# First output projection: four pairs of modulation weights loaded first, the embeddings in other memory, and eight gate products moved under layer A's output tiles

## What is computed

```
y = concat([y_h, y_f])                        # 1024 + 1024 wide
h = x + y @ w_out                             # the first output projection
h = h + sigmoid(h @ w_ple_gate) * (p @ w_ple) # p: embeddings, 256 wide
h = rmsnorm(h, final_norm_w)
for layer i in (A, B):
    shift, scale, gate = split(silu(c) @ w_ada[i] + b_ada[i])          # for the tokens
    shift_c, scale_c, gate_c = split(silu(c_ctx) @ w_ada[i] + b_ada[i])# for the context
    u = h * (1 + scale) + shift
    h = layer_norm(ALPHA * h + gate * mixer_i(u), ...)
```

## Time and profile before

| | us |
|---|---|
| median of 3 runs | 3524.75 |
| lowest, highest | 3517.57, 3527.97 |
| the profiled execution's own time | 3509.49 |
| its span | 3507.7 |
| TensorE busy | 3189.2 (91%) |
| VectorE busy | 2024.5 (58%) |
| first output projection, first group of tiles | 1320.7 to 1410.4 |
| second group | 1425.1 to 1515.6 |
| embeddings' product | 1546.0 to 1569.8 |
| gate product starts | 1571.25 |

### The profile page before, as it was taken

One profiled execution on the slowest core, in us unless ns is written; L12 is line 12 of the kernel. 1 busy time (PEld: TensorE's weight loads), 2 busy tenths in 40 slices (PEclk: granted clock), 3 DMA queues, 4 the chain that ended last, 5 costly groups with the idle time before them and its releaser, 6 DMA issues.

```text
span 3507.7 us, 49113 instructions
## 1 busy us (share of the span) xinstructions
PE 3189.2 (91%) x18168; PEld 2659.5 (76%) x18168; DVE 2024.5 (58%) x3865; ACT 1288.3 (37%) x2277; POOL 877.3 (25%) x324
## 2 busy tenths in 40 slices
PE   7999999899999989869799989999779999999986
PEld 6878888777777768657588878887657777777765
DVE  4766657555566555965655545544455555555543
ACT  3433343344444440022344434430134444554402
POOL 2554444422222223334110010003111111111120
PEclk8999999999999999989899999999689999999996
DMA  2111111111111136541200010042021111110321
GB/s 98 52 39 45 36 39 41 65 44 65 49 54 49 55 144 252 191 142 44 97 34 28 28 40 28 28 167 91 12 77 47 41 47 47 41 35 31 119 96 60
DMA packets 64695, 236.95 MB, mean 68 GB/s; under 512 B 7024, under 2 KB 10096, under 8 KB 63488
## 3 DMA queue, kind: packets, MB, share of 16 engines
q1 hardware_dynamic: 31680, 115.91, 9.2%
q10 hardware_dynamic: 32832, 118.58, 9.1%
HBM read 184.06 MB, written 50.40 MB: 67 GB/s over the span
## 4 chain that ended last, share of the span: by engine, by line
PE 66%; DVE 16%; issue 5%; DVEq 5%; ACT 4%; DMA 2%; ACTq 1%; POOLq 1%; POOL 0%; SPq 0%
PE ps L1124 20%; PE ps L165 19%; PE ps L1189 4%; PE ps L1155 4%; PE ps L1171 4%; PE ps L727 3%; PE ps L120 3%; DVE x_in L1647 2%; PE ps L704 2%; DVEq L526 2%; PE ps L361 1%; DVE fox_l L1276 1%; PE ps L688 1%; DVE ctx_in L1647 1%; DVE h_sb L1647 1%
## 5 line engine op out<-in xcount | busy, mean ns | idle before, releaser
L186 POOL TENSOR_TENSOR w_hi<-raw,small 128x1024 fp32r<-128x1024 f32 x160 | 453.9, 2837 | 2528.8 <-PE ps L165 1335.5
L188 POOL TENSOR_TENSOR w_lo<-raw,w_hi 128x1024 fp32r<-128x1024 f32 x160 | 423.7, 2648 | 22.8
L1124 PE MATMUL ps<-nb_u_hi,w_hi 128*128 128x512 f32 (+1 forms) x640 | 252.0, 394 | 21.6 <-DVE nb_q_lo L2185 12.1
L1124 PE MATMUL ps<-nb_u_hi,w_lo 128*128 128x512 f32 (+1 forms) x640 | 248.2, 388 | 0.0
L1124 PE MATMUL ps<-nb_u_lo,w_hi 128*128 128x512 f32 (+1 forms) x640 | 247.2, 386 | 0.0
L1287 DVE TENSOR_TENSOR nb_pt_lo<-ps,nb_pt_hi 128x512 fp32r<-128x512 f32 x208 | 143.8, 691 | 143.0 <-ACT nb_pt_hi L1214 142.7
L165 PE MATMUL ps<-u_hi,w_hi 128*128 128x512 f32 x528 | 213.3, 404 | 7.8 <-DVE u_lo L245 7.8
L1124 PE MATMUL ps<-u_hi,w_hi 128*128 128x512 f32 x512 | 209.7, 410 | 4.5 <-POOL w_lo L188 4.5
L1124 PE MATMUL ps<-u_hi,w_lo 128*128 128x512 f32 x512 | 210.1, 410 | 0.0
L165 PE MATMUL ps<-u_hi,w_lo 128*128 128x512 f32 x528 | 210.0, 398 | 0.0
L1124 PE MATMUL ps<-u_lo,w_hi 128*128 128x512 f32 x512 | 208.9, 408 | 0.0
(11 more groups left out here) (348 smaller groups left out, 8121.5 us busy)
## 6 DMA issues: line engine op xcount, KB each, us to landing
raw<-in_w_stream SPq DMA_DIRECT2D x160, 512.0 KB, 3.2
h_sb<-in_w_ada ACTq DMA_DIRECT2D x12, 1024.0 KB, 4.8
ctx_in<-in_w_ada ACTq DMA_DIRECT2D x12, 1024.0 KB, 4.8
nf_b<-nf_rows ACTq DMA_DIRECT2D x16, 512.0 KB, 4.4
nb_bias<-in_rel_bias ACTq DMA_DIRECT2D x16, 448.0 KB, 3.6
y_parts<-wa_y_hi ACTq DMA_DIRECT2D x8, 640.0 KB, 3.0
y_parts<-wa_y_lo ACTq DMA_DIRECT2D x8, 640.0 KB, 4.1
la_out_yh<-y_parts SPq DMA_DIRECT2D x8, 640.0 KB, 10.0
```

The source lines that it names most:

```text
L186: pool.tensor_tensor(w_hi[:, s, :], raw[:, s, :], zero, ALU.add)
L188: pool.tensor_tensor(w_lo[:, s, :], raw[:, s, :], w_hi[:, s, :].bitcast(F32), ALU.subtract).then_inc(w_ready, 1)
L1124: mm = pe.matmul(ps[:, b:b + ch["n"]], w(slot, k), u[:, k, ch["c0"]:ch["c0"] + ch["n"]], start=k == 0 and p == 0, stop=k == KT - 1 and p == 2)
```

## The change

- The weights' pairs in the first projection are 20 instead of 24 (units 0 to 39). Pairs 0 to 3 are loaded at once into four slots, all in `h_sb`, pairs 4 to 15 into `h_sb[4:6]` and `h_sb[6:8]`, and pairs 16 to 19 into memory of `y_hi0`/`y_lo0` (a new view `rows4`), which ScalarE's queue may fill when the second group's HGRN tiles are done (`U_OUT + 12`). `cond` moves to the context's memory.
- For pairs 0 to 15 only the reductions for i = 0 are preceded by a drain. Pairs 16 to 19 keep both.
- `OUT1_ORDER`: additions 0 to 3 after 9, 10, 11 and 12 pairs, additions 4 to 7 after 16, 17, 18 and 19. `p_lo` is made before addition 6.
- `p` is loaded behind pair 15 into `r_hi[6:8]`'s memory. `p_hi` is `r_lo[4:6]` and `p_lo` is `r_lo[6:8]`, so VectorE's `r_lo[4]` to `r_lo[7]` wait for the embeddings' product (before: two of them).
- Units 40 to 47 (layer B's gates, i = 0) become eight reductions in `Layer.dve` of layer A, two each ahead of tiles 2, 3, 5 and 6. ScalarE's queue loads silu's input (0.5 MB) and two blocks of 2 MB for them, into memory that was a gap.

```diff
-        cond = h_sb[:, 4:6, :]
-        ada_pairs = [h_sb[:, 6:8, :], p_in.rearrange("p (u n) -> p u n", u=2)]
-        PAIRS_ADA = ADA_UNITS // 2
+        cond = ctx_in[:].rearrange("p k t -> p (k t)").rearrange("p (i n) -> p i n", i=2)
+        PAIRS_ADA = 20
         OUT1_ORDER = [("pair", p) for p in range(PAIRS_ADA)]
-        for k, pairs_before in enumerate((9, 10, 12, 13)):
-            OUT1_ORDER.insert(pairs_before + k, ("add", k))
-        OUT1_ORDER += [("add", k) for k in range(4, KT)]
+        for p, k in ((19, 7), (18, 6), (17, 5), (16, 4), (12, 3), (11, 2), (10, 1), (9, 0)):
+            OUT1_ORDER.insert(p, ("add", k))
+        OUT1_ORDER.insert(OUT1_ORDER.index(("add", 6)), ("low", 0))
...
+        p_raw = rows4[:, KT - 2:KT, :]
+        p_hi = r_lo[:, KT - 4:KT - 2, :]
+        p_lo = r_lo[:, KT - 2:, :]
+        def ada_pair(p):
+            if p >= 16:
+                return rows4[:, KT + 2 * (p % 2):KT + 2 * (p % 2) + 2, :]
+            first = (4, 6, 0, 2)[p] if p < 4 else (4, 6)[p % 2]
+            return h_sb[:, first:first + 2, :]
...
-            load_pair(0)
-            load_pair(1)
+            for p in range(4):
+                load_pair(p)
...
+                if what == "pair":
+                    nxt = {0: 4, 1: 5, 2: None, 3: None}.get(n, n + 2)
+                    if nxt and nxt < PAIRS_ADA:
+                        act.wait_ge(ada_done, n + 1)
+                        load_pair(nxt)
+                    if n == 15:
+                        act.dma_start(p_raw, a["p_t"]).then_inc(p_loaded, 16)
+                elif what == "add":
+                    if n + 1 < KT:
+                        act.wait_ge(o_added, n + 1)
+                        load_x(n + 1)
+                    if n == 4:
+                        act.wait_ge(p_loaded, 16)
+                        nc.scalar.copy(p_hi, p_raw).then_inc(p_hi_set, 1)
...
-                        for i, out in outs if 2 * n + j < ADA_UNITS - KT else outs[:1]:
-                            dve.drain()
+                        for i, out in ((0, x_in[:, 1, :]), (1, w if n < 16 else x_in[:, 1, :])):
+                            if i == 0 or n >= 16:
+                                dve.drain()
...
-                if k == KT - 2:
+                if k == KT - 4:
                     dve.wait_ge(w_used, U_PLE + 2)
...
+                residual(0)
+                if self.l == 0:
+                    act.dma_start(self.cond[:], a["cond"][0:1, :].broadcast_to([P, D])).then_inc(cond_loaded, 16)
+                    next_ada(0)
+                    act.wait_ge(cond_loaded, 48)
+                    nc.scalar.activation(self.cond[:], self.cond[:], ACT.Silu).then_inc(cond_set, 1)
+                residual(1)
+                if self.l == 0:
+                    next_ada(1)
...
+                    for j in range(2):
+                        w = self.ada_w[:, 2 * (step % 2) + j, :]
+                        dve.drain()
+                        ins = dve.tensor_tensor_reduce(self.ada_x[:], w, self.cond[:], 1.0, small[:, 0:1], ALU.mult,
+                                                       ALU.add, ada[:, 40 + 2 * step + j, 0:1])
...
+                    if l == 0 and k in (2, 3, 5, 6):
+                        dot_gates((2, 3, 5, 6).index(k))
                     dve.wait_ge(self.chunk, (k + 1) * (len(self.chunks) - 1) + 2 * self.base)
```

More of the change, by code:

```diff
@@ L1369, in build_program @@
         cond_loaded = sem("cond_loaded")
-        ada_loaded = [sem("ada_loaded0"), sem("ada_loaded1")]
+        ada_loaded = [sem(f"ada_loaded{i}") for i in range(4)]
         ada_done = sem("ada_done")
@@ L1549, in modulation @@
             ln_b = vecs[:, V_LNB:V_LNB + KT].unsqueeze(2).broadcast_to([P, KT, 2])
+            if l == 1:
+                units = slice(24, 40)
             dve.tensor_tensor(adv[:, units], ada[:, units], vecs[:, V_BADA:V_BADA + ADA_UNITS][:, units].unsqueeze(2)
-                              .broadcast_to([P, 24, 2]), ALU.add)
+                              .broadcast_to([P, units.stop - units.start, 2]), ALU.add)
             if l == 0:
@@ L1613, in out1_act @@
             for what, n in OUT1_ORDER:
[L1614 to L1634, removed]
+                if what == "pair":
[12 more added lines that the diff above has]
+                        nc.scalar.copy(p_hi, p_raw).then_inc(p_hi_set, 1)
         def out1_dve(dve):
-            dve.memset(ada[:, ADA_UNITS - KT:, 1], 0.0)
             dve.wait_ge(cond_set, 1)
@@ L1649, in out1_dve @@
                     ins.then_inc(ada_done, 1)
-                    if (n + 1) % 12 == 0:
+                    if n == 11:
                         dve.drain()
-                        modulation(dve, n // 12)
+                        modulation(dve, 0)
+                elif what == "low":
+                    dve.wait_ge(p_hi_set, 1)
+                    dve.tensor_tensor(p_lo, p_raw, p_hi.bitcast(F32), ALU.subtract).then_inc(p_lo_set, 1)
                 else:
                     i, m = n // 4, n % 4
-                    if n == KT - 1:
-                        low_embeddings(dve)
-                    dve.wait_ge(x4_loaded[x_slot(n)], 16 * sum(x_slot(k) == x_slot(n) for k in range(n + 1)))
+                    dve.wait_ge(x4_loaded, 16 * (n + 1))
                     dve.wait_ge(o_chunk, 8 * i + 4 + m + 1)
                     dve.wait_ge(w_used, 8 * i + U_OUT + 4 + m + 1)
-                    dve.tensor_tensor(h_sb[:, n, :], bank(2 * m, 2), x_in[:, x_slot(n), :], ALU.add).then_inc(o_added, 1)
+                    dve.tensor_tensor(h_sb[:, n, :], bank(2 * m, 2), x_in[:, 0, :], ALU.add).then_inc(o_added, 1)
+            dve.drain()
+            modulation(dve, 1)
         def ple_pe(pe):
@@ L1850, in residual, with next_ada @@
                         act.dma_start(self.res[:, m, :], h_dram[i * 2 + m, :, 0:self.cols]).then_inc(self.res_loaded, 16)
-                for i in range(KT // 2):
-                    residual(i)
+                def next_ada(i):
+                    act.wait_ge(ada_done, PAIRS_ADA + 2 * i)
+                    act.dma_start(self.ada_w[:], a["w_ada"][40 + 4 * i:44 + 4 * i].rearrange("u p n -> p u n")
+                                  ).then_inc(ada_loaded[i], 16)
+                residual(0)
[7 more added lines that the diff above has]
+                    next_ada(1)
+                residual(2)
+                residual(3)
                 for k in range(KT):
@@ L1864, in dve, with dot_gates @@
                 dve.memset(self.acc[:], 0.0)
+                def dot_gates(step):
+                    if step == 0:
+                        dve.wait_ge(cond_set, 2)
+                    dve.wait_ge(ada_loaded[step // 2], 16 * (PAIRS_ADA // 4 + 1))
+                    for j in range(2):
+                        w = self.ada_w[:, 2 * (step % 2) + j, :]
+                        dve.drain()
+                        ins = dve.tensor_tensor_reduce(self.ada_x[:], w, self.cond[:], 1.0, small[:, 0:1], ALU.mult,
+                                                       ALU.add, ada[:, 40 + 2 * step + j, 0:1])
+                    ins.then_inc(ada_done, 1)
+                    if step == 3:
+                        dve.drain()
+                        dve.tensor_tensor(gates[:, 1, :, 0], ada[:, 40:48, 0], vecs[:, V_BADA + 40:V_BADA + 48], ALU.add)
+                        dve.drain()
                 for k in range(KT):
```

33 lines of the change are left out of this document (18 added, 15 removed).

## The result

| | before | after |
|---|---|---|
| median of the runs (4 each) | 3521.16 | 3476.28 |
| lowest, highest | 3517.57, 3527.97 | 3473.82, 3483.36 |
| the profiled execution's own time | 3509.49 | 3473.82 |
| its span | 3507.7 | 3472.0 |

The ratio is 0.9874 [0.985, 0.9897], so the changed kernel is 1.3% (44.9 us by the medians) faster. A second set (a_again, four runs of the changed kernel) gave 3477.63 against 3516.78 and a ratio of 0.9893 [0.9878, 0.9908] (39.2 us). The forecast was 3484 (3473 to 3498), a gain of 40.7. It was taken from the median of three runs, 3524.75; from the 3521.16 of four it would be 3480.5.

A forecast was written before the change was run, and what follows sets the result against it. VectorE's chain of 88 reductions was taken to cause TensorE's 14.7 and 30.5 us waits. Gate product 43.3 us earlier, less 2.0 stalls and 0.6 load, gives 40.7: from the median 3524.75 to 3484 us, range 3473 to 3498.

The forecast's parts named there:

- wait for y at the first fox tile: First group: the earlier pairs delay y by 5.1 us, so TensorE waits 3.2 to 4.5 us, taken as 4.0.
- lost to the clock behind it: Behind TensorE's wait for y the granted clock falls, losing 1.3 to 2.2 us, taken as 1.9.
- first addition done: VectorE in the first projection: the first addition ends at 1412.4 instead of 1425.0 on the old trace's clock.
- wait ahead of the second group: TensorE's 14.7 us wait goes: the first group ends at 1416.3, later than the first addition at 1412.4.
- wait for `p_lo`: Ahead of the embeddings' product: TensorE's 30.5 us wait is gone, with 6 us to spare.
- embeddings' product starts: The second group ends at 1504.3 instead of 1515.6; the product then runs at full clock and ends at 1526.5 instead of 1569.8.
- stalls in its first pair of tiles: Gate product: four `r_lo` tiles wait for the embeddings' product instead of two, a stall of 0 to 3.8 us, taken as 2.0.
- layer A's block load longer by: Layer A's output: 2.6 MB loaded beside the last input block, on which TensorE waits, costs 0.6 us.
- stage and load, gain: Whole sum: gate product 43.3 us earlier, less 2.0 of stalls and 0.6 of load, gives 40.7 us.
- the forecast's rival: VectorE's reductions: the flush comes anyway, so a pair stays at 5.6 us and the first addition comes 2.0 us later.
- The rival in which VectorE stays the bound: Second group: pairs slip 0.4 to 1 us each, first addition no sooner than 1425.1; gain 29.5 us, 3495; chance 0.17.
- the bound of 6.4 by bytes in order: Layer A's block load: if all 2.6 MB went ahead of it at 410 GB/s, it would cost 6.4 us.

The follow-up runs named there:

- b_again: The kernel before, unaltered, traced once more; one run, 3510.05 us.
- a_all_drains: The changed kernel with a drain ahead of every reduction of the first projection again; median 3481.53 us, ratio to before 0.9910.
- a_no_gates: The changed kernel without layer B's eight gate reductions and their loads, gates set to one, so it computes something else; 3475.58 us, ratio to before 0.9885.
- a_gates_back: The changed kernel with layer B's eight gate products back in the first projection as pairs 20 to 23, behind all others; 3499.18 us, ratio to before 0.9951.
- b_four_first: The kernel before with four pairs loaded first, pairs 2 and 3 in `h_sb[0:4]`, and nothing else; 3505.97 us, ratio to before 0.9969.
- b_fewer_drains: The kernel before with the drain ahead of the i = 1 reductions left out, nothing else; 3515.04 us, ratio to before 1.0001.
- a_best: The changed kernel with pairs 0 to 2 ahead of y, pair 3 behind it, and addition 0 after eight pairs instead of nine; 3484.95 us, ratio to before 0.9909.
- a_three_first: The changed kernel with pairs 0 to 2 loaded ahead of y and pair 3 right behind it; 3483.97 us, ratio to before 0.9911.

## Why the prediction was right, step by step

| step | predicted | measured |
|---|---|---|
| wait for y at the first fox tile | 4.0 (3.2 to 4.5) | 5.0 |
| lost to the clock behind it | 1.9 | 1.8 |
| hole ahead of pair 4 | about 9 | 8.9 |
| first addition done | 91.7 | 90.5 |
| wait ahead of the second group | 0 | 0 |
| `p_lo` done, on the old clock | 1498 | 1494.8 |
| wait for `p_lo` | 0 | 0 |
| embeddings' product starts | 183.6 | 184.4 |
| gate product starts | 207.3 | 208.0 |
| stalls in its first pair of tiles | 2.0 | 2.4 |
| second pair starts | 232.7 | 233.9 |
| layer A's block load longer by | 0.6 | 0.1 |
| stage and load, gain | 40.7 | 40.0 |

*y.* TensorE waited 5.0 us and not 4.0, past the range of 3.2 to 4.5. The 4.0 was a delay of 5.1 less a cover of 1.1. The cover was right: in the profile before, the last load of y (issued at 27.7 us from the first tile) landed at 44.5 and the first fox tile began 1.2 us later, in b_again 1.0. The delay was too small: in the changed kernel that load was issued at 34.0 and landed at 50.6, so it was 6.1 us late for 2.1 MB more ahead of it. The forecast also had the four pairs landed at 22.3; the last landed at 27.5, which cost nothing, as VectorE took it up only at 38.6. Pair 4 landed 5.3 us later than pair 2 had, as forecast. Why y lost 1 us more than its bytes isn't shown. This 1 us is the largest miss among the waits. The clock did what the nearest rows said: the twelve units took 133.7 us against 12 x 10.99 = 131.9.

*The drains.* The undrained distance is 1.21 and the drained 1.40, as the earlier trace rows had it. The Trainium skill (VectorE: DVE Perf Modes, The DRAIN you can't avoid) has a flush behind every operation that chaining doesn't skip, and the forecast's rival took from it that both distances are 1.40. The same section adds that a next operation that isn't held starts earlier. For this pair of instructions the trace decides: the explicit drain is what costs the 0.19. It didn't matter to the time in the changed kernel, as a_all_drains shows.

*The second group* began behind TensorE's own first group and not behind the addition. Pair 6 waited 0.3 us and pair 15 2.4 for their weights, so the loads came just in time for VectorE. The rival in which VectorE stays the bound did not come, with ten microseconds of cover at `p_lo` where I had six.

*The gate product.* The three waits for `r_lo` are 3.3 us in the list of waits, and the first pair takes 2.4 more than its 23.39 before. VectorE shows where it comes from: four `r_lo` tiles take 8.5 us, two of them on GpSimd's split, as counted from the earlier trace rows.

```profile
1525.86 8.52 DVE L1709 TENSOR_TENSOR r_lo<-h_sb,r_hi 128x1024 fp32r<-128x1024 f32 x4 [2.98 <-PE ps L165]
```

*Layer A's load* took 8.27 (8.25 and 8.01 in the other two traces) against 8.02 and 8.16. 2.6 MB more on ScalarE's queue cost SyncE's block at most 0.25 us. The rule of the Trainium skill that was weighed there (DMA: Bandwidth & Descriptors, Arbitration) fits this, and the bound of 6.4 by bytes in order is excluded.

*What each part brings*, taken away from the changed kernel at the last marks: the gate products 23 us, the order of additions 16, the early pairs 7, the drains none. The sum is more than 40 because taking away either of the first two alone makes TensorE wait on VectorE's chain again. Put alone on the kernel before, the early pairs bring 10. The embeddings' new place and their earlier load stayed in all of these versions of the changed kernel, so what they bring alone was not tested.

**Where the two profiles lose 6 us.** At the last mark the changed kernel is 1.5 + 40.1 = 41.6 us ahead. When layer A's block has landed it is 37.8 ahead, at the end of layer A's sums 34.9, and at the end 35.7. The first 2 us of it are lost at the first 144 matmuls in a row of layer A, and there the kernel before shows the same in its second trace. The rows are from the profile before, b_again and the profile after; over their first 5 us the granted clock is 1.00, 0.68 and 0.61.

```profile
1731.87 27.70 PE ps L165 x144
```

```profile
1730.94 29.41 PE ps L165 x144
```

```profile
1690.71 29.77 PE ps L165 x144
```

The chain of layer A's output in the changed kernel:

```profile
2321.88 8.27 DMA la_out_yl<-y_parts
...
2350.81 28.00 PE ps L165 x144
...
2380.89 28.00 PE ps L165 x144
...
2410.98 29.27 PE ps L165 x144
```

A pair of tiles takes 28.0 or 29.3. Before, all three were 27.7 to 28.0 in both traces. In a_again two are slow. These are its stretches behind the wait of 2.1 us ahead of each, then those of the kernel before:

```profile
2346.79 29.57 PE ps L165 x144
...
2378.44 29.23 PE ps L165 x144
...
2409.75 28.00 PE ps L165 x144
```

```profile
2348.00:2353.00 5.00, 5.00 (x20) 4.19 (x19) 4.78 (x3) 0.00 (x0) 2.35 (x1) 0.70 0.77 266
2353.00:2358.00 5.00, 5.00 (x28) 4.27 (x27) 1.41 (x4) 0.00 (x0) 0.00 (x0) 1.00 0.25 101
...
2378.00:2383.00 5.00, 4.56 (x15) 3.80 (x16) 4.82 (x3) 0.00 (x0) 3.87 (x2) 0.66 0.70 238
2383.00:2388.00 5.00, 5.00 (x28) 4.30 (x27) 0.36 (x1) 0.00 (x0) 0.00 (x0) 1.00 0.58 240
```

```profile
2387.40:2392.40 5.00, 4.99 (x25) 4.23 (x26) 4.86 (x2) 0.00 (x0) 3.51 (x1) 1.00 0.52 171
...
2417.40:2422.40 5.00, 4.91 (x25) 4.20 (x26) 4.91 (x2) 0.00 (x0) 3.54 (x2) 1.00 0.49 183
```

The granted clock falls to 0.70 and 0.66 over five microseconds in one and stays at 1.00 in the other, behind the same wait. I had first blamed the eight reductions in layer A. But a_no_gates and a_gates_back have no such work in layer A and show it: 29.56, 29.56, 28.01 in the one, and in the other

```profile
2375.48 29.27 PE ps L165 x144
...
2406.84 29.30 PE ps L165 x144
...
2438.23 29.30 PE ps L165 x144
```

b_four_first (29.46 to 29.49, all three) and b_fewer_drains (28.00, 28.00, 29.30) show it with layer A as it was. So it isn't the change's work in that place. Each of the other kernels has some of it there, and the kernel before, in two traces, has none. Why a wait of 2.1 us costs 1.5 more in some executions and nothing in others stays open.

Counted from the first output tile, all three traces of the changed kernel lose something behind the last mark: 40.1 ahead of the profile before at that mark, they are 34.2, 34.0 and 30.3 ahead at the end (b_again: 0.0). b_four_first goes from 10.4 to 2.9 in the same way. The executions also differ: the profile before lies 11.7 us below the median of its set, and only 2 of 53 other runs of that kernel were shorter, where the profile after lies 2.5 below its own. That is the whole difference between 35.7 and 44.9.

The medians of the three sets of runs gave 36.6, 39.2 and 44.9 for the whole, so the forecast's sum of 40.7 lies among them, and this piece is about as large as the runs' own scatter.

## What to carry to other kernels

When one engine's long list of small works ends in a product that another waits for, look first at which of it isn't needed there: eight of 88 reductions moved beneath later tiles were worth more (22 us) than a faster start (7 to 10) or cheaper instructions (nothing measurable). Follow all that the next product needs, also through a third engine's queue: addition 7 came in by ScalarE's copy, which undid a_best, and in a_gates_back loads queued ahead of that copy held TensorE for 20.8 us though all additions were done.

## What was unexpected of the hardware

- The granted clock fell behind some waits of about 2 us and not behind others. In a_three_first it was 1.00 behind 2.3 us and 0.66 behind 1.9. In layer A's output the same 144 matmuls took 27.7 or 29.5 us behind a wait of 2.1, and behind the gate product's three stalls the clock was 1.00 or 0.68.
- One core's loads held 408 to 410 GB/s over 33 us, before and after (1333 to 1366).
- One execution (b_fewer_drains) had a mean granted clock of 0.93 against 0.95 from 60 to 600 us and was 8 us later at the projection, with the same code up to there.
- The explicit drain costs 0.19 us per reduction, and the reduction that writes over its own weights takes the same 1.28 us as the one that doesn't. A reduction that falls on GpSimd's split takes 2.5 to 3.4.
